# The recurrence of an RWKV layer: both sides of each triangular inverse in different halves of the partitions

## The chip, the cores and the metric

One core of one Trainium2 chip. The time is the device time of one execution in microseconds, lower is better. TensorE (PE) multiplies and transposes; VectorE (DVE), ScalarE (ACT) and GpSimd (POOL) work elementwise; SyncE (SP) issues most DMAs. All data is float32. SBUF has 128 partitions; results of TensorE land in PSUM, 8 banks of 512 columns per partition.

## The reference, cut to what matters

The whole model is a gated MLP layer with a mixture of experts, an RWKV layer with another, and two attention layers. The change touches only the recurrence of the RWKV layer, 512 tokens behind a context of 256, 16 heads of 64, forward and backward in time:

```python
def _wkv_step(S, inp):
    r_t, w_t, k_t, v_t, a_t, b_t = inp
    sa = jnp.einsum('zbhvk,zbhk->zbhv', S, a_t)
    S = S * w_t[..., None, :] + sa[..., :, None] * b_t[..., None, :] + v_t[..., :, None] * k_t[..., None, :]
    return S, jnp.einsum('zbhvk,zbhk->zbhv', S, r_t)
```

## The kernel before, in words

The 768 steps are cut into 12 chunks of 64 tokens. Inside a chunk the steps become products of 64x64 matrices, of which one is the inverse of a unit triangular matrix 1 - L. From chunk to chunk only a linear step of the 64x64 state is left.

`recurrence` (L1269) works two heads at a time (128 channels fill the 128 partitions), in eight calls of `two_heads`. Each call runs three streams of work, interleaved by hand:

- **`chunks` (L1648)**, the matrices of this pair of heads, in three rounds of two tiles of 128 tokens: round 0 the context (tiles 4 and 5, without outputs), rounds 1 and 2 the latent tiles. A round covers 2 directions x 2 tiles x 2 chunks x 2 heads = 16 matrices of 64x64. `units` are the four (direction, tile), `quads` the four (head, chunk).
- **`Prepare` (L1317)**, for the next pair: small products with the LoRA weights, sigmoids, cumulated sums, exponentials, normalised keys. Each engine has a generator of steps (`on_tensor`, `on_scalar`, `on_vector`, `on_pool`), and `chunks` takes one step at each `next(ahead)`.
- **`Scan` (L1539)**, for the pair before: 12 state steps (`next(behind)`), then y is transposed, copied by ScalarE (L1633) and stored by SyncE (L1578).

The first call has no scan, the last no preparation; `Prepare.alone` comes before all, `Scan.alone` after. Every engine executes its own list in order, so a step that waits holds up all that is queued behind it. `Turns` only counts semaphores. At the end of a call all engines meet, and semaphores are cleared.

A round of `chunks`: the products P1 (L and r by b, L1707), XA (L transposed, L1713) and P2 (with k, L1719) go to PSUM and are masked by VectorE (L1832, L1836, L1840). GpSimd masks out of L the quarter of level 1 (L1925) and of level 0 (L1926), and adds the identity (L1929) to both sides of the inverse, `XX`: side 0 holds X, side 1 its transpose. Then five levels double the size of the inverted blocks, 2 to 64. In each, per head:

- Z = quarter of L by X, 8 products (L1745), copied out by ScalarE (L1891, a helper at L1875);
- the update, X side 0 by Z (L1753) and Z by X side 1 (L1756), 8 products each, in level 5 only the second;
- VectorE adds the result to both sides (L1847).

Meanwhile GpSimd makes the quarters two levels ahead (L1934). A product of two 64-row operands uses one 64x64 tile of the array; which one is set by the half of the partitions that its operands lie in and the half that its result goes to. Before, a chunk `cc` of a tile keeps to its own half throughout (`row[cc]`), so operands and result lie in the same half. Ahead of the levels stand the transposes of a and b (L1727) and M.V (L1733); behind them those of k (L1774), then W and U (L1781, copied by ScalarE), Q (L1789), G (L1796, L1798), y's part inside the chunk (L1806, L1808) and F (L1815). VectorE scales Q and G (L1856, L1859) and adds the identity to F (L1866). The scan's step is 4 products of F and the state (L1593), taken up by L1619, and 4 that read y (L1601, added at L1628).

In the profile a float32 product counts as two records of MATMUL and two of LDWEIGHTS (8 products are "x16"); a transpose is one.

## Time and profile before

| | |
|---|---|
| runs | 4815.3, 4812.1, 4813.68 us; median 4813.68 |
| the profiled execution | 4814.21 us, its span 4812.3 us |
| granted clock of TensorE, mean | 0.895 |
| TensorE busy | 3984.3 us (83%) |
| VectorE, ScalarE, GpSimd busy | 1266.8, 819.4, 557.9 us |
| the eight calls of `two_heads` | from 2083.8 to about 2906 us of the span |

The span is from the first to the last instruction of the program in the profile; the time of an execution has little around it. "L1745" is line 1745 of the kernel. An idle time stands in brackets with the one that ended it; "issue" is time in which the engine waited for nothing that the profile shows. The granted clock is a share of 2.4 GHz, the other level is 1.2 GHz.

### The profile page before, as it was taken

Reading aid. Unit: us, or ns where it says so; the run is one execution under the profiler, and the core shown is the slowest. Engines: PE = TensorE matmul, PEld = TensorE weight load, DVE = VectorE, ACT = ScalarE, POOL = GpSimd, SP = SyncE. Lnnn points to the kernel's source line nnn. Section 1 sums busy time; section 2 is a strip of 40 time slices with the busy share of each in tenths; the row PEclk is TensorE's granted clock in tenths of the full one; section 3 lists DMA queues with packets and bytes.
Section 4 is the critical chain, followed back from the end, with each engine's and each line's share of the span. In section 5 each row is a group of like instructions: output and inputs, shape, how many; then the busy total and the mean of one; then the engine's idle time right before and its main releaser. Section 6 shows DMA issues by size and latency. Waiting matters only on the chain. (4 is left out here: it accounts for less than half of the span.)

```text
span 4812.3 us, 71623 instructions
## 1 busy us (share of the span) xinstructions
PE 3984.3 (83%) x30390; PEld 2332.4 (48%) x30390; DVE 1266.8 (26%) x2657; ACT 819.4 (17%) x1707; POOL 557.9 (12%) x718
## 2 busy tenths in 40 slices
PE   4599993699999469878888887579999939997787
PEld 1245542344444235557777773334444414464454
DVE  0213102100000250055455554310000020252174
ACT  0101001011111010143333421001111110231142
POOL 0000000110110000054443530011111100000000
PEclk8799995799999779989999997689999979857999
DMA  8411114388888432200000002348888823201100
GB/s 348 180 53 61 48 35 150 122 331 328 319 330 326 154 90 90 71 14 16 27 16 16 16 6 111 133 177 328 331 318 329 331 102 93 83 1 45 35 36 22
DMA packets 284408, 676.85 MB, mean 141 GB/s; under 512 B 23693, under 2 KB 46829, under 8 KB 283500
## 3 DMA queue, kind: packets, MB, share of 16 engines
q1 hardware_dynamic: 255260, 586.42, 33.6%
q0 software_dynamic: 20928, 71.68, 3.9%
q10 hardware_dynamic: 7952, 14.81, 0.8%
q8 instruction: 213, 3.49, 0.3%
q14 instruction: 55, 0.45, 0.0%
HBM read 618.19 MB, written 54.77 MB: 140 GB/s over the span
## 5 line engine op out<-in xcount | busy, mean ns | idle before, releaser
L862 PE MATMUL banks<-w_gate_ring,x_turned 128*128 128x512 f32 x1024 | 460.0, 602 | 15.3 <-DVE x_turned L934 15.3
L891 PE MATMUL banks<-w_down_ring,hidden_turned 128*128 128x512 f32 x1024 | 450.1, 592 | 1.4 <-ACT hidden_turned L915 1.4
L869 PE MATMUL banks<-w_up_ring,x_turned 128*128 128x512 f32 x1024 | 449.9, 592 | 0.0
L891 PEld LDWEIGHTS banks<-w_down_ring,hidden_turned 128*128 128x128 f32 x1024 | 194.4, 190 | 245.8 <-issue 243.9
L869 PEld LDWEIGHTS banks<-w_up_ring,x_turned 128*128 128x128 f32 x1024 | 194.6, 190 | 244.9 <-issue 244.9
L862 PEld LDWEIGHTS banks<-w_gate_ring,x_turned 128*128 128x128 f32 x1024 | 190.7, 191 | 247.2 <-issue 216.3
L945 DVE COPY y_out_rows<-banks 128x512 f32<-128x512 f32 x64 | 44.3, 692 | 890.9 <-PE banks L891 890.9
L345 PE MATMUL banks<-const_cols,h_tokens 128*128 128x128 f32 x240 | 54.0, 404 | 221.9 <-DVE h_tokens L328 147.0
L1847 DVE TENSOR_TENSOR inverse_both_ways<-banks,inverse_both_ways 128x512 f32<-128x512 f32 (+1 forms) x240 | 152.3, 637 | 252.1 <-PE banks L1756 251.2
L1745 PE MATMUL banks<-inverse_both_ways,l_quarters 64*64 64x64 f32 x3840 | 150.1, 224 | 32.0 <-POOL inverse_both_ways L1929 24.2
L438 PE MATMUL banks<-gmlp_weights,h_turned_gmlp 128*128 128x512 f32 x384 | 166.5, 596 | 11.1 <-DMA gmlp_weights<-in_ga_w_in_dram 11.1
L580 PE MATMUL banks<-gmlp_weights,u_channels 128*128 128x512 f32 x384 | 165.1, 592 | 0.8 <-DVE u_channels L546 0.8
L458 PE MATMUL banks<-h_turned_gmlp,gmlp_weights 128*128 128x384 f32 x512 | 165.3, 486 | 0.0
L1264 PE MATMUL banks<-mixed,proj_weights 128*128 128x384 f32 x512 | 165.3, 486 | 0.0
L345 PEld LDWEIGHTS banks<-const_cols,h_tokens 128*128 128x128 f32 x240 | 44.4, 213 | 234.1 <-DVE h_tokens L328 156.8
L1745 PEld LDWEIGHTS banks<-inverse_both_ways,l_quarters 64*64 64x64 f32 x3840 | 129.9, 136 | 57.4 <-POOL inverse_both_ways L1929 27.3
L843 POOL DMA_INDIRECT y_rows<-y_out_rows,put_rows x64 | 63.2, 987 | 802.8 <-DVE y_out_rows L945 802.8
L939 DVE TENSOR_TENSOR hidden<-silu_gate,banks 128x512 f32<-128x512 f32 x64 | 44.0, 687 | 414.4 <-PE banks L869 414.4
L1756 PE MATMUL banks<-inverse_both_ways,step 64*64 64x64 f32 x3840 | 152.8, 220 | 0.3
L1875 ACT ACTIVATE step<-banks 128x256 f32<-128x256 f32 x240 | 92.2, 384 | 271.1 <-PE banks L1745 265.7
L1756 PEld LDWEIGHTS banks<-inverse_both_ways,step 64*64 64x64 f32 x3840 | 132.4, 136 | 3.2 <-ACT step L1875 2.6
L857 PE MATMUL banks<-const_cols,x_rows 128*128 128x128 f32 x512 | 68.2, 277 | 78.5 <-DMA x_rows<-h_rows,take_rows 78.5
(429 smaller groups left out, 5692.0 us busy)
## 6 DMA issues: line engine op xcount, KB each, us to landing
w_gate_ring<-in_moe_w_gate_dram SPq DMA_DIRECT2D x64, 2048.0 KB, 14.2
w_up_ring<-in_moe_w_up_dram SPq DMA_DIRECT2D x64, 2048.0 KB, 14.4
w_down_ring<-in_moe_w_down_dram SPq DMA_DIRECT2D x64, 2048.0 KB, 9.7
ada_ring<-in_ada_w_dram SPq DMA_DIRECT2D x12, 4096.0 KB, 23.6
gmlp_weights<-in_ga_w_in_dram SPq DMA_DIRECT2D x8, 2048.0 KB, 8.0
ab_weights<-in_ab_w_in_dram SPq DMA_DIRECT2D x6, 2048.0 KB, 8.6
y_back<-y_rows SPq DMA_DIRECT2D x10, 1024.0 KB, 5.2
gmlp_weights<-in_ga_w_out_dram SPq DMA_DIRECT2D x4, 2048.0 KB, 8.1
```

Of the source, the lines that this page charges most:

```text
L345: last = pe.transpose(core.ps[:, 2 * (j % 2) + half, k * P:(k + 1) * P], h[:, j % 2, c0:c0 + P], core.c("ident"))
L438: last = pe.matmul(core.ps[:, step % 8, :], hT[:, k, t * P:(t + 1) * P], wring[:, i % 2, k, :], start=k == 0, stop=k == KD - 1)
L458: last = pe.matmul(core.ps[:, (step + 4) % 8, 0:TOK], wring[:, i % 2, k, m * P:(m + 1) * P], hT[:, k, half * TOK:(half + 1) * TOK], start= ...
L580: last = pe.matmul(core.ps[:, bank, :], uT[:, rest * KD + k, t * P:(t + 1) * P], wring[:, rest, k, :], start=rest == 0 and k == 0, stop=re ...
L862: last = pe.matmul(ps[:, G, :], xT[:, r, k, :], wg[:, r, k, :], start=k == 0, stop=k == KD - 1)
L869: last = pe.matmul(ps[:, U, :], xT[:, r, k, :], wu[:, r, k, :], start=k == 0, stop=k == KD - 1)
L891: last = pe.matmul(ps[:, Y + half, :], hT[:, k, :], wd[:, r, k, half * HALF:(half + 1) * HALF], start=k == 0, stop=k == KF - 1)
L1264: last = pe.matmul(ps[:, i % 8, 0:HT2], wring[:, n % 2, k, m * P:(m + 1) * P], mix[:, j % 2, k, half * HT2:(half + 1) * HT2], start=k == 0 ...
L1745: last = pe.matmul(ps[row[cc], 4 * h + 1, u * CHUNK:(u + 1) * CHUNK], LQ[h][row[cc], n % 2, u, :], XX[h][row[cc], 0, u, :], start=True, st ...
L1756: last = pe.matmul(ps[row[cc], 4 * h, (4 + u) * CHUNK:(5 + u) * CHUNK], Z[h][row[cc], u, :], XX[h][row[cc], 1, u, :], start=True, stop=True)
L1847: DVE.mark(dve.tensor_tensor(x, ps[:, 4 * h, at], x, ALU.add), by_dve, f"XX{n}_{h}")
L1875: copy = lambda dst, src: act.activation(dst, src, ACT.Copy)
```

## The change

In head `h` and chunk `cc`, L and side 0 of the inverse now lie in the half `to_row(h, cc) = row[cc ^ h]`, side 1 and Z in the other, `from_row`. The first product of an update then crosses from one half to the other, the second stays, and with both chunks the four tiles are used in turn. Side 1 gets its product in bank 4h+1, side 0 in bank 4h. L, X and its transpose come from three sets of products (XL, XA, XM). ScalarE copies L unmasked, and GpSimd makes all five masked quarters at the start of a round, each in a buffer of its own. The level-0 inverse is not built: `XI` keeps the identity from the first call on, and VectorE overwrites the entries of the level-0 quarters alone, with predicated copies. r by b becomes products of its own beside level 1, masked after level 2. Other work moves between the levels: a transposed by products with the identity (level 1), b and k transposed (level 3), M.V (level 4). W and U are four tiles wide and copied by two engines. F is copied without the identity, and the scan adds the state by products with the identity (`unit`). In the calls the scan reads y into the free half of bank 3, and `Prepare` keeps to bank 7, one product at a time. Its steps are dealt anew to the levels, and the copy of y for the store comes last on ScalarE. The core of the diff ("..." marks what is left out):

```diff
 class Prepare, on_tensor
+        lag = 2 if self.spare != 7 else 1
         ...
-                if n or z:
-                    pe.wait_ge(s["sig_done"], 2 * (2 * n + z))
                 for half in range(2):
-                    pe.matmul(ps[:, 2 + 4 * half, 0:H2], w[part, :], ...
-                yield
+                    done = 4 * n + 2 * z + half
+                    if done >= lag:
+                        pe.wait_ge(s["sig_done"], done - lag + 1)
+                    pe.matmul(ps[:, (7, self.spare)[half], 0:H2], w[part, :], ...
+                    yield
         ...
-        for t in range(NTA):
-            last = pe.transpose(ps[:, 2 + 4 * (t // 3), ...
+        for half in range(2):
+            if half:
+                pe.wait_ge(s["kk_unit"], 1)
+            for t in range(NTA // 2):
+                ...
+            yield
 class Scan, on_tensor
                     for h in range(2):
-                        last = pe.matmul(ps[row[h], 3, z * CHUNK:(z + 1) * CHUNK], b["F"][row[h], z, ch, :], S[row[h], z, j % 2, :], start=True, stop=True)
+                        pe.matmul(ps[row[h], 3, at], b["F"][row[h], z, ch, :], S[row[h], z, j % 2, :], start=True, stop=False)
+                    for h in range(2):
+                        last = pe.matmul(ps[row[h], 3, at], self.unit[row[h], :], S[row[h], z, j % 2, :], start=False, stop=True)
 chunks
+        to_row = lambda h, cc: row[cc ^ h]
+        from_row = lambda h, cc: row[cc ^ h ^ 1]
 on TensorE
+                    wait(by_act, ACTS, "YC", 1)
+                    ... XA: ps[to_row(h, cc), 4 * h + 1, u * CHUNK:(u + 1) * CHUNK], a by b
+                    ... XM: ps[from_row(h, cc), 4 * h + 1, (4 + u) * CHUNK:(5 + u) * CHUNK], b by a
                     wait(by_dve, DVE, "QG", 1)
+                    ... XL: ps[to_row(h, cc), 4 * h, u * CHUNK:(u + 1) * CHUNK], b by a
+                    wait(by_act, ACTS, "F", 1)
                     ... P2, as before
                     for n in lv:
+                        X = XI if n == 1 else XX
                         for h in range(2):
+                            wait(by_dve, DVE, f"XM_{h}" if n == 1 else f"XX{n - 1}_{h}")
+                            wait(by_pool, POOL, f"LQ{n}_{h}")
                             for u in range(4):
                                 for cc in range(2):
+                                    last = pe.matmul(ps[from_row(h, cc), 4 * h + 1, u * CHUNK:(u + 1) * CHUNK], LQ[h][to_row(h, cc), n - 1, u, :],
+                                                     X[h][to_row(h, cc), 0, u, :], start=True, stop=True)
+                        if rnd == 0 and n < 5:
+                            next(ahead, None)
                         for h in range(2):
                             wait(by_act, ACTS, f"Z{n}_{h}")
                             for u in range(4):
                                 for cc in range(2):
+                                    here = from_row(h, cc)
+                                    if n < last_lv:
+                                        pe.matmul(ps[to_row(h, cc), 4 * h, u * CHUNK:(u + 1) * CHUNK], X[h][here, 1, u, :], Z[h][here, u, :], start=True, stop=True)
+                                    last = pe.matmul(ps[here, 4 * h + 1, (4 + u) * CHUNK:(5 + u) * CHUNK], Z[h][here, u, :], X[h][here, 1, u, :], start=True, stop=True)
+                        if n == 1:
+                            ... (waits MR_0, MR_1; a by identity, and if lat b by r: 16 products each) TA
+                        if n == 3:
+                            ... (waits TA copied, RB) transposes of b into bank 2: TB; of k into bank 6: TK
+                        if n == 4:
+                            ... (waits TK copied) MV, from row[cc] to from_row(h, cc)
                         next(behind, None)
+                        if (rnd == 0 and n < 5) or (rnd == 1 and n in (1, 3, 4)):
                             next(ahead, None)
+                    ... WU, 16 products from from_row(h, cc) to row[cc]
+                    if rnd == 2:
+                        next(ahead, None)
+                    wait(by_act, ACTS, "WU_0")
+                    wait(by_dve, DVE, "WU_1")
                     ... Q, G, YC, F as before (RB in place of LR)
 on VectorE
+                if not scan:
+                    for h in range(2):
+                        dve.tensor_copy(XI[h][:, :, :, :].rearrange("p a u c -> p (a u) c"), c_("ident64").unsqueeze(1).to_broadcast([P, 8, CHUNK]))
                     for h in range(2):
+                        dve.wait_ge(products, PE.of("XM", rnd))
+                        DVE.mark(dve.copy_predicated(by_dir(XI[h][:, 0, :, :]), both("x0", 2, CHUNK).bitcast(U32), by_dir(fours(ps[:, 4 * h + 1, low]))), by_dve, f"XA_{h}")
+                        DVE.mark(dve.copy_predicated(by_dir(XI[h][:, 1, :, :]), both("q1_0", 2, CHUNK).bitcast(U32), by_dir(fours(ps[:, 4 * h + 1, high]))), by_dve, f"XM_{h}")
                     ...
+                        if n == 2 and lat: (waits TA copied) RB: two masked products of 256 columns
                         next(behind, None)
-                        if (rnd, n) not in IDLE:
+                        if (rnd == 0 and n > 2) or (rnd == 1 and n > 1) or rnd == 2:
                             next(ahead, None)
+                    dve.wait_ge(products, PE.of("WU", rnd))
+                    DVE.mark(dve.tensor_copy(WU[:, :, :, 1, :], ...), by_dve, "WU_1")
                     ... QG as before, next(ahead); the sum of F and identity gone
 on ScalarE, per round: L_0, L_1 copied; per level Z_0, Z_1, then TA (n=1), TB and TK (n=3), MV (n=4),
+                        next(ahead, None)
+                        if rnd == 0 and n < 5:
+                            next(ahead, None)
+                    ... WU_0, YC, F copied
+                    if rnd < 2:
                         next(ahead, None)
                 run(ahead)
+                if scan:
+                    scan.on_scalar(act)
 on GpSimd
                 for rnd, pair in enumerate(PAIRS):
+                    for n in lv:
+                        for h in range(2):
+                            pool.wait_ge(by_act, ACTS.of(f"L_{h}", rnd))
+                            POOL.mark(pool.tensor_tensor(by_dir(LQ[h][:, n - 1, :, :]), by_dir(L[h][:, :, :]), quarters(n), ALU.mult), by_pool, f"LQ{n}_{h}")
+                    for _ in range((1, 5, 3)[rnd]):
                         next(ahead, None)
```

## Rows read from the trace of the kernel before

**Rows 1.** Windows of two calls: us; busy PE, PEld, DVE, ACT, POOL; granted clock; DMA.

```profile
2501.00:2606.70 105.70, 91.34 (x2538) 81.42 (x2539) 54.76 (x127) 40.96 (x84) 45.01 (x51) 0.95 0.06 18
...
2816.80:2906.00 89.20, 78.63 (x2496) 73.08 (x2496) 40.60 (x108) 23.94 (x59) 28.40 (x42) 0.98 0.02 7
```

**Rows 2.** Timeline: start us, us, engine, line, operation; round 1, up to level 2.

```profile
2539.27 0.86 PEld L1707 LDWEIGHTS banks<-a_and_r,b_scaled 64*64 64x64 f32 x32 [0.22 <-DVE state_addend L1859]
...
2542.17 0.74 DVE L1836 TENSOR_TENSOR inverse_both_ways<-banks,scan_masks 128x256 f32<-128x256 f32 x2
...
2542.47 0.42 PEld L1727 LDWEIGHTS banks<-const_cols,a_and_r 128*128 128x128 f32 x4
...
2544.36 0.64 POOL L1925 TENSOR_TENSOR l_quarters<-l_and_rb,scan_masks 128x256 f32<-128x256 f32 x1
...
2546.81 0.55 PEld L1745 LDWEIGHTS banks<-inverse_both_ways,l_quarters 64*64 64x64 f32 x16 [1.63 <-POOL inverse_both_ways L1929]
...
2550.56 1.01 PEld L1745 LDWEIGHTS banks<-inverse_both_ways,l_quarters 64*64 64x64 f32 x32 [0.17 <-issue]
```

**Rows 3.** Timeline of the last call: a level without preparation.

```profile
2863.43 0.54 PEld L1753 LDWEIGHTS banks<-step,inverse_both_ways 64*64 64x64 f32 x16
...
2864.63 0.69 DVE L1847 TENSOR_TENSOR inverse_both_ways<-banks,inverse_both_ways 128x512 f32<-128x512 f32 x1 [1.23 <-PE banks L1756]
...
2865.29 0.32 PEld L1593 LDWEIGHTS banks<-state,state_factor 64*64 64x64 f32 x8
...
2865.76 1.09 PEld L1745 LDWEIGHTS banks<-inverse_both_ways,l_quarters 64*64 64x64 f32 x32
...
2866.49 0.38 ACT L1875 ACTIVATE step<-banks 128x256 f32<-128x256 f32 x1 [2.57 <-PE banks L1745]
...
2866.93 1.09 PEld L1756 LDWEIGHTS banks<-inverse_both_ways,step 64*64 64x64 f32 x32
```

**Rows 4.** Timeline of a middle call: W and U, then Q and G.

```profile
2565.28 1.72 PEld L1781 LDWEIGHTS banks<-a_and_mv,inverse_both_ways 64*64 64x64 f32 x32 [0.17 <-issue]
...
2567.94 0.56 PEld L1789 LDWEIGHTS banks<-l_and_rb,w_and_u 64*64 64x64 f32 x32 [0.94 <-ACT w_and_u L1875]
...
2568.40 0.21 PEld L1796 LDWEIGHTS banks<-w_and_u,b_tokens 64*64 64x64 f32 x8
```

**Rows 5.** Timeline of round 0 of the same call: levels 2 and 3.

```profile
2513.14 1.74 PEld L1745 LDWEIGHTS banks<-inverse_both_ways,l_quarters 64*64 64x64 f32 x32 [0.55 <-issue]
...
2517.92 1.55 PE L1390 MATMUL banks<-decay_lora,lora_w 64*128 64x384 f32 x4
...
2519.40 1.01 PEld L1745 LDWEIGHTS banks<-inverse_both_ways,l_quarters 64*64 64x64 f32 x32 [0.55 <-issue]
```

**Rows 6.** Timeline of the same call: steps of the preparation.

```profile
2531.90 1.50 PE L1395 MATMUL banks<-scan_masks,x_tokens 128*128 128x2 f32 x12
...
2533.61 1.02 ACT L1428 ACTIVATE x_tokens<-a_gate,params_here 128x768 f32<-128x768 f32 x1
...
2552.16 1.28 ACT L1439 ACT_TABLE_LOAD   x1
...
2558.61 2.59 DVE L1489 TENSOR_TENSOR k_scaled<-x_tokens,exp_minus_cum 128x768 f32<-128x768 f32 x1
```

**Rows 7.** Timeline: from round 1 to round 2.

```profile
2571.97 0.27 PE L1806 MATMUL banks<-l_and_rb,w_and_u 64*64 64x64 f32 x1 [1.59 <-issue]
...
2572.55 0.90 PEld L1707 LDWEIGHTS banks<-a_and_r,b_scaled 64*64 64x64 f32 x32
```

**Rows 8.** Timeline: end of the same call, start of the next.

```profile
2602.20 0.65 PE L1815 MATMUL banks<-b_tokens,w_and_u 64*64 64x64 f32 x32
...
2606.68 0.33 SPq L1373 DMA_DIRECT2D x_tokens<-k_channels  x1
```

**Rows 9.** DMA issues: count, KB each, median us from issue to landing.

```profile
y_rows_rwkv<-y_two_heads SPq DMA_DIRECT2D x8, 256.0 KB, 2.3
```

**Rows 10.** Timeline: a state step of the scan alone.

```profile
2914.34 0.51 PEld L1593 LDWEIGHTS banks<-state,state_factor 64*64 64x64 f32 x8 [0.34 <-DVE state L1619]
```

More of the change, by code:

```diff
@@ L1729, in _ @@
-                    for h in range(2):
-                        wait(by_dve, DVE, f"MR_{h}")
-                        for u, (z, ti) in enumerate(units):
-                            for cc in range(2):
-                                last = pe.matmul(ps[row[cc], 4 * h + 2, u * CHUNK:(u + 1) * CHUNK], MR[h][row[cc], u, 0, :],
-                                                 b["V"][row[cc], pair[ti], h * 64:(h + 1) * 64], start=True, stop=True)
-                        PE.mark(last, products, f"MV_{h}")
@@ new lines, in _ @@
+                        if n == 4:
+                            wait(by_act, ACTS, "TK")
+                            for u, (z, ti) in enumerate(units):
+                                for h, cc in quads:
+                                    last = pe.matmul(ps[from_row(h, cc), 4 * h + 2, u * CHUNK:(u + 1) * CHUNK], MR[h][row[cc], u, 0, :],
+                                                     b["V"][row[cc], pair[ti], h * 64:(h + 1) * 64], start=True, stop=True)
+                            PE.mark(last, products, "MV")
@@ L1785, in _ @@
-                    wait(by_act, ACTS, "WU_1")
+                    for h in range(2):
+                        wait(by_dve, DVE, f"XX{last_lv}_{h}")
+                    wait(by_act, ACTS, "MV")
+                    for u in range(4):
+                        for h, cc in quads:
+                            here = from_row(h, cc)
+                            last = pe.matmul(ps[row[cc], 4 * h + 1, u * P:(u + 1) * P], XX[h][here, 1, u, :],
+                                             AM[h][here, u, :, :].rearrange("p a c -> p (a c)"), start=True, stop=True)
```

305 lines of the change are left out of this document (147 added, 158 removed).

## The prediction

> **What bounds the kernel now.** The windows by call come first: a middle call of `two_heads` lasts 105.7 us with TensorE busy 91.3, VectorE 54.8, ScalarE 41.0 and GpSimd 45.0 [rows 1]. Eight such calls and the two stretches alone make some 885 us of the 4812.3 us span; nothing else is touched. A matrix engine that is busy 86% of a call invites counting columns, so I read the timeline next, to see what each group of products waits for. A level without preparation takes 3.50 us from one update to the next [rows 3]: Z of both heads (from 2865.76, 0.47 us a head), the first head's update 1.17 us after Z began (Z, then ScalarE's copy), both updates 4 x 0.465 = 1.86 us, then the scan step 0.47. TensorE is never idle in it; VectorE's two additions lie beside it. So **inside a level the issue of products binds**, and at the seams (start of a round, W and U, end of a call) a chain over three engines does.
>
> **Durations.** I sum against the profiled execution (span 4812.3, its own time 4814.2); the median of three is 4813.7, 0.5 less, and I use the difference. What a measurement of this kernel can tell from no change is about 0.2%, some 10 us.
>
> **The update.** Products whose operands and results stay in one half of the partitions use two of the four 64x64 tiles and go at 0.47 us for 16 records (two records are one product); those that use all four go at 0.46 us for 32 (2567.94 to 2568.40) [rows 4]. After the change Z is still two wide (both heads use the same two tiles) and the update four wide for levels 1 to 4; level 5 has only the diagonal pair. The level becomes: Z to first update 1.17; the second head's update can't start before its own copy (0.54 later, 1.71); its issue 0.47; the scan step grows from 16 records to 24 by the unit products, 0.70. Sum 2.88, so 0.62 saved, not the 0.93 that the columns say: ScalarE's copy of the second head ends last. VectorE (first addition 0.73 after the update's issue ends its rows, 0.69 each [rows 3]) frees Z at 2.65, in time.
>
> The Trainium skill (TensorEngine Tiling, Restrictions and Gotchas) says that different row tiles can't write one PSUM bank at once; here both row halves write bank 4h. Rows bear on it: the updates of before send both row halves to one bank at 1.86/64 = 0.029 us a record, while full 128-row products of 128 columns take 0.105 each, 0.053 for 64 [rows 2, 3]. Two row halves do share a bank as long as their output halves differ, which the new layout keeps. By the rule the update would stay at 0.93 a head; that is a rival below.
>
> **The seams of a round.** Before, from the first product to Z of the second head 7.54 us, to Z of level 2 11.29 [rows 2], with 1.6 us in GpSimd's quarter and identity additions. After: XA, XM, XL 3 x 0.47; ScalarE copies L at 1.7; the first quarter 0.64 on GpSimd ends at 3.0; VectorE's four predicated copies end by about 3.1. No row shows a predicated copy; the masked product out of PSUM of the same width takes 0.37 [rows 2], the addition over 512 columns 0.69 [rows 3]. I take 0.4, being the same shape and source; at 0.69 each round loses 1.2, 28 us in 24 rounds. Z begins at 3.05, the second at 3.7; update, a and r.b (0.93), scan step: Z of level 2 at 6.9. GpSimd makes all ten quarters by 9 us, ahead of each level, so these cost nothing unless the copy of L is late. Moved into levels: transposes of b and k (0.85) in level 3, M.V (0.47 after 1.14) in level 4. W and U: 1.72 to 0.86, two copies side by side instead of in a row, the k transposes out of the way: 2.66 becomes about 1.8 and 0.45 before it goes. The addition of the identity to F leaves VectorE; it was beside. A round with nothing prepared beside it, now (89.2 - 2.8)/3 = 28.8 (the last call less its end) [rows 1], is laid out anew as 6.9 to Z of level 2, 2.9, 3.7 and 3.3 for levels 2 to 4, and 7.5 from Z of level 5 to F's last product: 24.4 with rounding, **4.4 saved**.
>
> **The middle calls** hold preparation, whose steps were re-dealt. By round:
> - *Round 0*: now 38.2 us (2501.0 to 2539.3) [rows 1, 2]: 12.1 to Z of level 2, 6.3 for level 2, 19.9 the rest [rows 5]. After: level 1 still waits for the cleared state, then a and the table load (1.28) stand before the first sigmoid for which the second lora product waits: 11.2. Level 2: Z 0.93, lora 0.78, update 0.94, scan 0.3, lora 0.78: 3.7. Level 3 puts the copies of b and k (1.2) ahead of the sigmoid: 5.7; level 4 those of M.V: 5.3; level 5 and tail 7.1, the norm product (1.50) and its wait having left. Sum 33.0: -5.2.
> - *Round 1*: now 33.3, with 2.1 in which TensorE waits for nothing in the profile [rows 2, 7]. What is queued where: the norm product 1.4 now ends level 1 and holds Z of level 2; root and gate factor (0.27 + 1.02) sit before the copy of Z2: 0.8. Then ScalarE's widening of the norms (a like pass, 0.9) waits for VectorE's reciprocal, which stands behind both additions, r.b and the scan step of level 2, and **the copy of Z3 stands behind it**: 2.4. In level 3 copies and a factor: 0.3; in level 4 the copies of M.V, table load 1.28 and exp 0.84 delay Z5's copy: 1.4 [rows 6]. In level 5 VectorE's step precedes its copy of U: 1.3. 7.6 of waits, against seams, update and the normal-vector transposes saved (about 7): 33.8, +0.5.
> - *Round 2*: VectorE's steps of 0.95 follow the additions in all five levels; one beside GpSimd takes 2.59 [rows 6]. With r.b in level 2 the addition of level 3 waits 1.1 to 2.6; ScalarE's exps 1.3; the bonus product before Q 0.85. 25.5 and the same kind of wait 1.2, after 30.3 (2572.55 to 2602.85) [rows 7, 8]: -3.5.
> - *End*: the last products end at 2602.85, the next call begins at 2606.68: 3.8 [rows 8]. y's copy and store now follow F: result 0.2, F's two copies 0.8, y's copy 0.6 (as 0.38 for 256 columns [rows 3]), landing 2.3 [rows 9], then the reset of the semaphores, 2.6 as now: 6.5. **+2.7**. Before, the store lay under W and U.
>
> Sum -5.5 a call, six calls: -33. The first call (no scan, no store) -8. The last (no preparation) 3 x 4.4 - 2.7: -11. The scan alone has 11 state steps in one chain; 8 more records each, 0.4 by its groups of 8 [rows 10]: +4.4. Preparation alone: lora products overlapped -3.3, square late +0.9, halves in turn +0.9: -1.5. **Sum -49: 4765 us.** Unknown: predicated copies (0 to +28), stalls where TensorE waits for nothing in the profile, with a tenth more instructions (0 to +12), the re-dealt queues (-45 to +48).
>
> **Rivals.**
> 1. *The queues take turns well.* If the waits of rounds 1 and 2 (7.5 a call) hide, six calls give 45 more: 4720. For: ScalarE is busy 39% of a call. Against: an in-order queue is late wherever the wait stands. 0.15.
> 2. *ScalarE's queue becomes the chain*, the other side. Place: round 1, levels 1 to 4, copies of Z behind preparation. TensorE stops 2 to 3 us at a time; the granted clock was 0.95 over this call [rows 1], and in a stretch at the lower level (1.2 GHz) Z of both heads took 1.74 instead of 1.01, and level 2 of round 0 6.26 [rows 5]. If round 1 and part of round 2 run at that level, 8 more a call, 48 in six: 4813; from 8.2 a call more it is no gain. Range 4803 to 4835. For: the waits above come one after another, and the idle at a call's end grows by 2.7. Against: such low stretches last 4 us now. 0.20.
> 3. *The update is not four wide*, or the array does not use the diagonal and the crossed tiles together: the second update begins at 2.10 and a level takes 1.17 + 2 x 0.93 + 0.70 = 3.73 instead of 2.88, in 4 levels of 24 rounds 82, and W and U 0.86 x 24 = 20: 4867. Against: four-wide groups with the same mix of halves exist [rows 4]. The rule of the Trainium skill (TensorEngine Tiling, Restrictions and Gotchas) is one way to it. 0.05.
>
> **Numbers.** My case 0.60 (4740 to 4785), rival 1 0.15, rival 2 0.20 (0.05 faster, 0.08 within, 0.07 slower), rival 3 0.05. Faster 0.80, same 0.08, slower 0.12. The range goes from 4715 to 4812: it leaves out rival 3, the upper half of rival 2 and a little below rival 1.
>
> **What would show it.** Update groups of 32 records in about 0.5; bare levels in the last call 2.9; Z of level 2 about 7 after the round begins; in round 1 ScalarE's widening waiting on the reciprocal with Z3's copy behind; 6.5 from F to the next call; middle calls near 100, the last near 78. Middle calls at 94 would mean rival 1, at 105 rival 2; updates still 0.93 a head, rival 3. It would be wrong, too, if the predicated copies cost over 0.7.

## The result, and the profile after

The changed kernel takes 4865.5 us (median of four, 4856.2 to 4867.4) against 4814.5 before (4812.1 to 4823.5): a ratio of 1.0099, 95% interval 1.008 to 1.0117. It is **slower by 51 us**, where 49 us faster was forecast; the time lies above the range. The profiled execution took 4866.3, its span 4864.5, TensorE's mean granted clock 0.883 after 0.895.

The page first: busy time by engine and the slices of the span, then the queue that brings TensorE its instructions.

```profile
span 4864.5 us, 77050 instructions
...
PE 3955.8 (81%) x33046; PEld 2284.4 (47%) x33046; DVE 1259.4 (26%) x2667; ACT 830.4 (17%) x1779; POOL 475.1 (10%) x622
...
PEclk8799995799999789888898997679999979857999
...
q8 instruction: 234, 3.83, 0.3%
```

TensorE is busy 28 us less than before and has 2656 records more (two records are a product, and each has its weight load); the span is 52 us longer, so in sum its idle time grew by 81 us. The instruction queue moved 234 packets; before the change it moved 213. The 21 packets more fit the 5312 instructions that TensorE has more (2656 records and their loads) at 256 a packet.

I cut each call into rounds (first product of one to the first of the next) and the end (last product to next call). Means of the six middle calls, us:

| | before | forecast | after | sigmoids first | fast version |
|---|---|---|---|---|---|
| round 0 | 37.7 | 33.0 | **40.9** | 33.8 | 31.1 |
| round 1 | 32.9 | 33.8 | 34.9 | 35.1 | 34.6 |
| round 2 | 30.5 | 26.7 | 29.7 | 29.3 | 29.9 |
| end | 4.1 | 6.5 | 6.7 | 6.7 | 3.9 |
| middle call | 105.2 | 99.7 | **112.2** | 104.8 | 99.5 |
| first call | 101.5 | 93.5 | 104.8 | 92.5 | 93.4 |
| last call | 90.0 | 79 | 93.9 | 93.9 | 85.9 |

(The last two columns are experiments, below: a_sigmoid_first, and the version with three things put back, by its run v_again.) The forecast missed by 12.5 in each of six middle calls (75), 11 in the first and 15 in the last, 101 in all: the whole of the 100 us. Round 0 holds 7.9 of the 12.5, round 2 holds 3.0.

**The level did what was forecast.** ScalarE's copies of Z in the last call, a level without preparation (timeline, ScalarE alone):

```profile
2867.74 0.87 ACT L1917 ACTIVATE step<-banks 128x256 f32<-128x256 f32 x2 [1.05 <-PE banks L1763]
2870.41 0.38 ACT L1917 ACTIVATE step<-banks 128x256 f32<-128x256 f32 x1 [1.81 <-PE banks L1763]
```

2.67 us from level to level (forecast 2.88, before 3.50 [rows 3]); the 64 records of both updates took 1.18 from first start to last end. This is the shortest of the levels of that call. From Z to the next Z, levels 2, 3 and 4 of the last call's three rounds take 3.3, 3.9 and 3.4 us in the mean, where 2.9, 3.7 and 3.3 were laid out. VectorE's predicated copies:

```profile
2633.67 0.44 DVE L1869 COPY_PREDICATED inverse_of_pairs<-scan_masks,banks 128x256 f32<-128x256 uint32 x1 [1.80 <-PE banks L1740]
2634.01 0.43 DVE L1871 COPY_PREDICATED inverse_of_pairs<-scan_masks,banks 128x256 f32<-128x256 uint32 x1
```

0.34 apart: the 0.4 of the sum was right.

**Round 0 did not.** One middle call, level 1 into level 2 (timeline, all engines):

```profile
2639.51 0.66 ACT L1917 ACTIVATE a_and_mv<-banks 128x256 f32<-128x256 f32 x2 [2.06 <-PE banks L1782]
...
2640.18 1.28 ACT L1427 ACT_TABLE_LOAD   x1
...
2640.58 0.28 PE L1611 MATMUL banks<-state,scan_masks 64*64 64x64 f32 x4
...
2641.48 0.58 ACT L1427 ACTIVATE log_decay<-banks,params_here 128x384 f32<-128x384 f32 x1
2642.11 0.50 PEld L1394 LDWEIGHTS banks<-decay_lora,lora_w 64*128 64x128 f32 x2 [1.39 <-ACT log_decay L1427]
2642.11 1.65 PE L1394 MATMUL banks<-decay_lora,lora_w 64*128 64x384 f32 x2 [1.25 <-ACT log_decay L1427]
...
2643.69 1.44 PE L1763 MATMUL banks<-inverse_both_ways,l_quarters 64*64 64x64 f32 x22
```

Read it from the PE row at 2642.11 upwards. The second lora product waits 1.25 us for the first sigmoid; that stands on ScalarE behind the copies of a and the table load; and Z of level 2 stands behind the lora product on TensorE. At that moment, 2642.1 us, the clock goes down. Windows of this call and of the stretches after it (us; busy PE, PEld, DVE, ACT, POOL; granted clock; DMA):

```profile
2631.60:2744.00 112.40, 87.85 (x2874) 74.62 (x2876) 53.35 (x129) 42.50 (x93) 34.80 (x39) 0.89 0.06 17
...
2636.00:2642.00 6.00, 4.11 (x145) 3.20 (x141) 2.15 (x6) 3.23 (x6) 4.95 (x9) 1.00 0.27 85
2642.00:2650.00 8.00, 7.89 (x117) 5.50 (x117) 1.38 (x2) 1.99 (x5) 0.00 (x0) 0.50 0.01 2
2650.00:2659.00 9.00, 9.00 (x112) 6.28 (x114) 1.86 (x4) 2.05 (x5) 0.00 (x0) 0.50 0.01 2
```

At 0.50 (1.2 GHz) TensorE is busy 9.00 us of 9.00 with 112 records: levels 2 to 4 have become TensorE's own time at half the clock. Inside the eight calls the lower level lasts 182 us, before 54; in round 0 of a middle call 17 us, before 6. Calls of the same code differ by it, since one escaped the long stretch (the first row; the other shows a call that did not):

```profile
2523.20:2631.60 108.40, 81.51 (x2870) 70.66 (x2871) 53.17 (x128) 42.19 (x93) 34.87 (x39) 0.96 0.07 18
2743.90:2858.40 114.50, 88.26 (x2870) 75.60 (x2870) 54.23 (x128) 42.34 (x93) 34.88 (x39) 0.87 0.06 17
```

**The seams stop in the middle of a group.** Last call: the products of y behind G; XM of the next round; the scan's step in level 1 of that round (timeline, TensorE among the others):

```profile
2912.85 0.28 PE L1842 MATMUL banks<-r_by_b,w_and_u 64*64 64x64 f32 x3
...
2915.05 0.28 PE L1842 MATMUL banks<-r_by_b,w_and_u 64*64 64x64 f32 x3 [1.92 <-issue]
```

```profile
2917.26 0.28 PE L1740 MATMUL banks<-a_and_r,b_scaled 64*64 64x64 f32 x3
2919.07 0.34 PE L1740 MATMUL banks<-a_and_r,b_scaled 64*64 64x64 f32 x8 [1.52 <-issue]
```

```profile
2924.72 0.22 PE L1609 MATMUL banks<-state,state_factor 64*64 64x64 f32 x1
...
2926.75 0.27 PE L1609 MATMUL banks<-state,state_factor 64*64 64x64 f32 x2 [1.81 <-issue]
```

Three records of one group, 1.92 us of nothing, three more of the same group: no semaphore stands between them and nothing in the profile ends the wait. Counted over the eight calls, such idle time (pieces over 0.35 us) is 57.8 us, before 15.3. The pieces stand 126 to 128 records apart, or a multiple of that: in the last call after records 655, 909, 1163, 1289, 1542, 1795, 1923, 2177, 2556 and 2811. A packet of the instruction queue is 3.83 MB / 234 = 16.4 kB; the Trainium skill (Perfetto Trace Analysis, The 4-stage abstract model) says that an instruction has 64 bytes, so a packet holds 256, and 127 records with their loads are 254 of them. The packets' own times tie the two together: 52 of the 55 pieces end 2.2 to 2.8 us after a packet began, where only some 12% of all records start that long after one; before the change it is all 15 pieces. So TensorE waits for its next packet. In no trace of this study do two packets start closer than 3.22 us, and in the last call they come 3.5 to 5.8 apart, 3.8 in the median. At the fastest of that call (254 records in 7.22 us between two pieces) a record with its load is supplied every 0.0285 us; two tiles wide they take 0.029, four wide 0.0146. I call this theory T1.

It is dear at the seams. "Z of level 2 about 7 after the round begins" was one of the prediction's signs (6.9 in its sum). In the last call it comes 8.5, 9.5 and 10.5 us after the start of rounds 0, 1 and 2, before the change 10.4, 9.6 and 9.7. In rounds 1 and 2 such pieces fill 2.3 and 3.3 us of it; without them it would be 7.2 both times.

**The end** is as forecast (TensorE's last product, y's copy, the store, the next call):

```profile
2737.54 0.66 ACT L1917 ACTIVATE state_factor<-banks 128x256 f32<-128x256 f32 x2 [1.47 <-PE banks L1850]
2738.09 0.60 ACT L1656 ACTIVATE y_two_heads<-banks 128x512 f32<-128x512 f32 x1
2738.78 0.37 SPq L1590 DMA_DIRECT2D y_rows_rwkv<-y_two_heads  x1
2743.88 0.33 SPq L1375 DMA_DIRECT2D x_tokens<-k_channels  x1
```

### The profile page after: what moved, and what is told of

Read it like the earlier page. It is cut to its first block and busy times, and to the rows that moved or that the text cites. A ratio compares the mean times of both kernels' runs of the same rounds, so it can differ in the third digit from the quotient of the medians.

```text
span 4864.5 us, 77050 instructions
## 1 busy us (share of the span) xinstructions
PE 3955.8 (81%) x33046; PEld 2284.4 (47%) x33046; DVE 1259.4 (26%) x2667; ACT 830.4 (17%) x1779; POOL 475.1 (10%) x622
## 3 DMA queue, kind: packets, MB, share of 16 engines
q8 instruction: 234, 3.83, 0.3%
## 5 line engine op out<-in xcount | busy, mean ns | idle before, releaser
L1977 POOL TENSOR_TENSOR l_quarters<-l_rows,scan_masks 128x256 f32<-128x256 f32 x240 | 144.2, 639 | 348.2 <-ACT l_rows L1917 348.2
L438 PE MATMUL banks<-gmlp_weights,h_turned_gmlp 128*128 128x512 f32 x384 | 167.7, 600 | 11.2 <-DMA gmlp_weights<-in_ga_w_in_dram 11.2
L1886 DVE TENSOR_TENSOR inverse_both_ways<-banks,inverse_both_ways 128x512 f32<-128x512 f32 x192 | 114.8, 621 | 209.1 <-PE banks L1775 208.0
L1775 PE MATMUL banks<-inverse_both_ways,step 64*64 64x64 f32 x3072 | 128.8, 238 | 7.4 <-ACT step L1917 6.9
L1763 PE MATMUL banks<-inverse_both_ways,l_quarters 64*64 64x64 f32 x3072 | 125.5, 234 | 8.8 <-issue 6.4
L905 ACT ACTIVATE x_turned<-banks 128x512 f32<-128x512 f32 x64 | 38.2, 597 | 542.4 <-PE banks L857 542.4
L1264 PEld LDWEIGHTS banks<-mixed,proj_weights 128*128 128x128 f32 x512 | 97.3, 190 | 68.1 <-issue 0.5
```

Of the source, the lines that this page charges most:

```text
L438: last = pe.matmul(core.ps[:, step % 8, :], hT[:, k, t * P:(t + 1) * P], wring[:, i % 2, k, :], start=k == 0, stop=k == KD - 1)
L1264: last = pe.matmul(ps[:, i % 8, 0:HT2], wring[:, n % 2, k, m * P:(m + 1) * P], mix[:, j % 2, k, half * HT2:(half + 1) * HT2], start=k == 0 ...
L1763: last = pe.matmul(ps[from_row(h, cc), 4 * h + 1, u * CHUNK:(u + 1) * CHUNK], LQ[h][to_row(h, cc), n - 1, u, :], X[h][to_row(h, cc), 0, u, ...
L1775: last = pe.matmul(ps[here, 4 * h + 1, (4 + u) * CHUNK:(5 + u) * CHUNK], Z[h][here, u, :], X[h][here, 1, u, :], start=True, stop=True)
L1886: DVE.mark(dve.tensor_tensor(flat(XX), sums, flat(XI if n == 1 else XX), ALU.add), by_dve, f"XX{n}_{h}")
L1977: POOL.mark(pool.tensor_tensor(by_dir(LQ[h][:, n - 1, :, :]), by_dir(L[h][:, :, :]), quarters(n), ALU.mult), by_pool, f"LQ{n}_{h}")
```

## The experiments

Ratios are to the kernel before on the same chip; idle by issue and time at the lower clock are sums inside the eight calls of the profiled execution, in us. (The expectation of a_filled says 188 us for the changed kernel: that takes whole stretches that begin in a call; inside the calls it is 182.)

| run | median us | ratio, 95% | idle by issue | lower clock |
|---|---|---|---|---|
| before | 4814.5 | 1 | 15 | 54 |
| the changed kernel | 4865.5 | 1.0099 (1.008 to 1.0117) | 58 | 182 |
| a_store_early | 4842.9 | 1.0048 (1.0031 to 1.0064) | 61 | 160 |
| a_identity_in_f | 4846.2 | 1.0062 (1.0045 to 1.0079) | 51 | 163 |
| **a_sigmoid_first** | 4814.5 | 0.9996 (0.9986 to 1.0005) | 58 | 88 |
| a_filled | 4840.3 | 1.0043 (1.0029 to 1.0057) | 67 | 100 |
| s_two_wide | 4879.3 | 1.0125 (1.0108 to 1.0142) | 31 | 87 |
| s_store | 4792.4 | 0.9937 (0.9924 to 0.995) | 56 | 98 |
| s_identity | 4786.7 | 0.9933 (0.9921 to 0.9945) | 57 | 70 |
| **s_store_identity** | 4771.1 | 0.9908 (0.9892 to 0.9925) | 55 | 53 |
| v_again, v_nops (same program) | 4773.2, 4770.7 | 0.9907, 0.9892 | 55, 52 | 63, 88 |
| v_a_turned | 4768.7 | 0.9891 (0.9877 to 0.9906) | 41 | 116 |
| v_sems | 5042.3 | 1.0466 (1.0452 to 1.048) | 215 | 394 |
| b_tiny | 5021.8 | 1.0417 (1.04 to 1.0435) | 7 | 180 |
| b_tiny_four | 4901.0 | 1.0167 (1.015 to 1.0184) | 19 | 91 |
| b_nops (same program as before) | 4817.1 | 0.9998 (0.9989 to 1.0008) | 18 | 54 |
| b_sems | 5095.2 | 1.0573 (1.0558 to 1.0587) | 188 | 246 |

### 1. ScalarE's order in round 0

> The changed kernel with one thing moved: in round 0 the first sigmoid of a level stands on ScalarE right behind the two copies of Z, ahead of the copies of a, of the tokens and of mv, so that TensorE's second lora product of the level does not wait behind them. Theory T2a (round 0 is late because the two halves of a lora product now share bank 7 and take turns with ScalarE behind the copies; levels 2 to 4 of round 0 take 8.1, 7.1 and 7.9 us in the middle calls, before 6.6, 5.7, 4.9): levels 2 and 4 lose 1 to 2 us each, 2 to 4 us a call, and where the clock then stays at its upper level up to 6; 15 to 35 us in all, to 4830 to 4850 us. Rival T1 (the supply of instructions sets these levels, the order on ScalarE is hidden): within 6 us of the changed kernel, the idle time by issue still near 58 us.

```diff
                             ACTS.mark(copy(Z[h]...), by_act, f"Z{n}_{h}")
+                        if rnd == 0 and n < 5:
+                            next(ahead, None)
                         if n == 1:
                             need("TA")
...
                         next(ahead, None)
-                        if rnd == 0 and n < 5:
-                            next(ahead, None)
```

One line's place gives all 51 us of the loss back: round 0 falls from 40.9 to 33.8 us, 0.8 from the forecast, and the lower clock from 182 to 88 us. The idle time by issue is 58 us as it was, so the rival is out for this part. (15 to 35 us were expected.) The rows that changed (ScalarE, then TensorE):

```profile
2602.72 1.28 ACT L1427 ACT_TABLE_LOAD   x1 [0.51 <-PE banks L1394]
2604.02 0.58 ACT L1427 ACTIVATE log_decay<-banks,params_here 128x384 f32<-128x384 f32 x1
2604.50 0.65 ACT L1917 ACTIVATE a_and_mv<-banks 128x256 f32<-128x256 f32 x2
```

```profile
2605.56 0.91 PE L1394 MATMUL banks<-decay_lora,lora_w 64*128 64x384 f32 x2
```

The table load now lies under TensorE's update and the lora product waits for nobody.

### 2. How much of that is the clock

> The changed kernel (sigmoids late, 4865 us) with six products of 128 columns by the identity put into TensorE's queue at the end of level 1 of round 0, just before the lora product that waits for the late sigmoid; nothing reads them. They fill the 1.25 us in which TensorE is idle there, right before the granted clock goes to its lower level for 13 to 17 us in most calls. If that idleness is what brings the clock down, and the clock what makes levels 2 to 4 late: clock at the lower level in the calls falls from 188 us to about 100, the middle calls from 112.2 to 107 to 109 us, 4825 to 4845 in all. Rival (levels 2 to 4 are late because of the order on ScalarE alone, and the clock falls behind it): the six products cost nothing or some 0.5 us a call, low clock stays near 188 us, 4860 to 4872.

```diff
                         next(behind, None)
+                        if rnd == 0 and n == 1 and prepare:
+                            pe.wait_ge(by_act, ACTS.of("TA", rnd))
+                            for _ in range(6):
+                                pe.matmul(ps[:, 2, 0:P], core.c("ident"), core.c("ident"), start=True, stop=True)
```

```profile
2632.57 1.60 PE L1810 MATMUL banks<-const_cols 128*128 128x128 f32 x12
2634.33 0.91 PE L1394 MATMUL banks<-decay_lora,lora_w 64*128 64x384 f32 x2 [0.16 <-ACT log_decay L1427]
```

Useless products in the place of the wait, with the late sigmoid left where it was: 25 us faster, the lower clock down from 182 to 100 us, middle calls 109.2. The idleness in front of the lora product does bring the clock down, and the clock alone is worth about half of the 51 us, 25 (27 by the ratios, uncertain by 11); the order on ScalarE keeps the other 26. Round 0 of the six middle calls, piece by piece, shows both (means, us; to Z of level 2, then from Z to Z, then the rest):

| round 0 | to Z of level 2 | level 2 | level 3 | level 4 | rest | sum |
|---|---|---|---|---|---|---|
| forecast | 11.2 | 3.7 | 5.7 | 5.3 | 7.1 | 33.0 |
| changed kernel | 12.7 | 7.0 | 8.2 | 5.6 | 7.3 | 40.9 |
| a_filled | 13.2 | 4.3 | 6.2 | 5.6 | 7.3 | 36.6 |
| a_sigmoid_first | 11.4 | 4.8 | 5.5 | 4.8 | 7.3 | 33.8 |

The clock is the 2.7 and 2.0 us of levels 2 and 3 that the useless products give back; the order is the 1.8, 0.7 and 0.8 us by which a_sigmoid_first is still shorter in front of Z of level 2 and in levels 3 and 4.

### 3. The store, and the identity

> The changed kernel with one thing put back: ScalarE copies the turned y after the levels of round 2, as before, and not behind everything else of the call. Theory T3 (the copy and the store of y stand bare at the end of each of the seven calls with a scan, 6.4 to 6.9 us from the last product to the next call against 3.9 to 4.3 before): the tail falls by about 2.5 us a call, in all 15 to 18 us, to 4847 to 4851 us. Rival (the tail is bound by something else, or round 2 pays for the copy in ScalarE's queue): no more than 5 us.

> The changed kernel with one thing put back: VectorE adds the identity to F, and a step of the scan is one product a half instead of two (88 records of TensorE less in each of seven calls). Theory T1 (TensorE is short of instructions: its groups of 256 instructions come no closer than about 3.65 us, and its idle time put down to issue rose from 15.3 to 57.8 us over the eight calls): 88 of the 332 added records go, so about a quarter of the 42 us of added issue time, 10 us, less what F's adds cost in round seams (2 copies of ScalarE change place with 2 adds of VectorE, about nothing): 4853 to 4860 us. Rival (products that stand in gaps cost nothing): within 4 us of the changed kernel.

> The changed kernel with the sigmoids first, and of the other two only the copy of y put back behind the levels of round 2. The clean price of T3 (the bare tail, 2.6 us in each of seven calls): 18 us less than with the sigmoids alone (0.9996 of before), so 0.9959 of before, 4798 us, range 4793 to 4804. Rival (the two put back at once gave 43 us, most of it through the tail): 4785 to 4792.

> The changed kernel with the sigmoids first, and of the other two only the identity back in F. By the difference of the runs so far, 43 less 18, it brings 25 us: 0.9948 of before, 4793 us, range 4787 to 4799. Theory T1 (it brings this through the supply of instructions) wants the idle time by issue down by about as much, from 58 to some 35 us. Rival (it brings it because a step of the scan stands in front of a level's products and is now 16 records shorter, 0.3 us or more in each of some twelve levels a call): idle time by issue stays at 50 to 58 us and the bare levels of the last call are shorter by 0.3 to 0.8 us.

```diff
+                    if rnd == 2 and scan:
+                        scan.on_scalar(act)
                     need("WU")
...
                 run(ahead)
-                if scan:
-                    scan.on_scalar(act)
```

```diff
-  pe.matmul(ps[row[h], 3, at], b["F"]..., S..., start=True, stop=False)
-  last = pe.matmul(ps[row[h], 3, at], self.unit[row[h], :], S..., start=False, stop=True)
+  last = pe.matmul(ps[row[h], 3, at], b["F"]..., S..., start=True, stop=True)
...
+  dve.wait_ge(products, PE.of("F", rnd))
+  last = dve.tensor_tensor(out["F"]..., by_dir(fours(ps[:, 4 * cc + 2, low])), c_("ident64")..., ALU.add)
```

On the changed kernel itself the two gave 23 and 19 us, but their clock moved at the same time (160 and 163 us at the lower level, after 182), so I repeated them on the version with the sigmoids first. There the store gives 0.0059 of the time, 28 us (18 expected; the interval reaches from some 20 to 36), and the identity 0.0063, 30 us (25 expected; some 23 to 38). The profiled executions differ by less, 17 and 23 us, and of the store's they show 2.9 us at the end of each middle call, which is what was expected; the rest of the 28 has no place in the traces. Idle by issue stays at 57 with the identity back: T1 wanted 35, and here the rival is right. The step of the scan stands in front of a level's products and is 8 records shorter (not 16, as the expectation has it). In the last call, where the clock is nearly the same (8.9 and 8.6 us at the lower level), the call is 3.7 us shorter and its idle time by issue only 0.4. ScalarE's copies of Z in its round 0 lie 4.4, 2.7, 4.1 and 3.8 us apart without, and 3.7, 2.7, 3.5 and 2.7 with the identity back: one of the four levels gains nothing. A part of the 30 us can be the clock (88 to 70 us).

> The changed kernel with the sigmoids first, the copy of y back behind the levels of round 2, and the identity back in F on VectorE: three put back at once. Alone they gave, against the changed kernel's 4865, 51, 23 and 19 us, in disturbed measurements of the last two (round 0's low clock came and went). If they add: 4865 - 51 - 18 - 18 = 4778 us, range 4768 to 4795, faster than before by 0.5 to 1%. If round 0 hid part of the two (they share its disturbance): 4795 to 4805.

All three put back: 4771.1 us, 0.9908 of before, **faster than both kernels**; it was run again (below). Middle calls take 99.7 us in this run and 99.5 in the next.

### 4. What four tiles wide is worth

> The changed kernel with the sigmoids first (4814.5 us), and in it the two sides of an inverse put back into the same half of the partitions: the updates and the products of w and u are two tiles wide again, all else as changed. Theory A (four tiles wide brings what was forecast, 0.6 us a level and 0.9 us for w and u): 15 levels and 3 seams in 8 calls give up 0.62 x 120 + 0.9 x 24, some 96 us, where nothing covers it: 4880 to 4915 us. Theory T1 (short supply of instructions takes back most of the gain; idle time by issue is 58 us in this kernel): two wide, a group is no faster than the supply, so the idle time by issue falls to 10 to 25 us and the net loss is 20 to 60 us: 4835 to 4875. Rival (the levels are bound by the copies and adds of other engines in most rounds): within 15 us of 4814.

```diff
-        to_row = lambda h, cc: row[cc ^ h]
-        from_row = lambda h, cc: row[cc ^ h ^ 1]
+        to_row = lambda h, cc: row[cc]
+        from_row = lambda h, cc: row[cc]
```

(The edit of experiment 1 is in it too.) 65 us slower than with the sigmoids first. The two expectations were 66 to 101 for A and 20 to 60 for T1; the run lies on the border, and the profile says why: idle by issue went from 58 to 31, at the same lower clock (88 and 87 us). The last call shows it best: 3.7 us longer, with 8.1 us less idle by issue. If all idle time by issue counts in full, which is not shown, four wide saves some 92 us and pays 27 of them back as waiting for instructions. Expectation A counted 120 levels, but level 5 is two wide in both; with 96 levels it is 81 us. So the gain of the update was no smaller than forecast, gross.

### 5. What an instruction costs

> The kernel before with 22 products of a single column and 32 weight columns put in behind the updates of every level (330 records a call, as many as the change adds to a middle call), where TensorE next waits for VectorE's add; their results are not used. Theory T1 (instructions come at a bounded rate): the extra records use up no array time to speak of, but push the groups of 256 instructions out: idle time by issue rises from about 15 us to 40 to 60 us over the eight calls, and the time by 20 to 45 us, to 4835 to 4860. Rival (instructions are free as long as TensorE waits anyway; the change costs for another reason): the 22 products take 0.3 to 0.6 us behind each update, inside a wait of over 1 us, and the time stays within 8 us of before.

> The kernel before with the same 22 single-column products behind each level's updates (each is two records, so 660 records a call, twice what the change adds; the expectation of the first such run counted them as 330), now dealt in turn to two halves of the rows and two of the columns of the array. In one place they took 0.035 us a record. Theory T1 (a burst faster than 0.0285 us a record empties TensorE's instructions): the burst takes less than 0.035 a record, idle time by issue rises from 15 to over 40 us, and a bare level is no shorter than its 140 records x 0.0285 = 4.0 us. Rival (a record costs its 0.035 us wherever it stands, TensorE's instructions are issued at that rate and no faster): 1.55 us a burst again, the time again near 5022 us, idle time by issue under 10 us.

```diff
+                        for k in range(22):
+                            rows, to = row[k % 2], slice(64 * (k // 2 % 2), 64 * (k // 2 % 2) + 32)
+                            pe.matmul(ps[to, 1 + 4 * (k % 2), 511:512], core.c("ident")[rows, 0:32], core.c("ident")[rows, 0:1], start=True, stop=True)
```

(The first of them had all 22 in one place of the array.) First row one place, second row four:

```profile
2906.58 1.55 PE L1759 MATMUL banks<-const_cols 64*32 64x1 f32 x44
```

```profile
2939.98 0.54 PE L1760 MATMUL banks<-const_cols 64*32 64x1 f32 x44
```

A record of one column is not free: 1.55 us for the 44, 0.035 each, in one tile, and 0.54 us, 0.012 each, dealt over four. The first run was expected to hide its products inside a wait of over 1 us; there is no such wait in a level, the update's end is the end of TensorE's time, and the bare levels grew from 3.3 to 4.9 us. It says nothing on T1, since its groups are slower than the supply and idle by issue fell to 7. The second refutes my stronger form of T1: idle by issue rose by 4 us only, not to 40, with bare levels of 3.9 us. Most bursts of 44 run through; 15 of the 120 are broken by an idle time "issue" (7.2 us in all). So a burst of 44 seldom empties what TensorE holds; the long pieces come in longer ones, as at the seams.

### 6. Fewer and more instructions in the fast version

> The version with all three put back (4771 us, 0.9908 of before), and in it a is turned by four transposes of a whole tile a round instead of by sixteen products with the identity: 84 records of TensorE less a call, 3% of them, and for one of the two heads in the wrong half of the partitions, so that w is not the reference's. Theory T1 (TensorE's groups of 256 instructions come no closer than 3.24 us in any kernel so far, mostly 3.6, and its idle time by issue is 55 us here): 84 records are 2.4 us of supply a call, the time falls by 8 to 19 us, to 4752 to 4763, and the idle time by issue by as much. Rival (the supply has room wherever it is not in a burst, and this group lies beside a wait): within 4 us of 4771.

```diff
-                                for h, cc in quads:
-                                    last = pe.matmul(ps[from_row(h, cc), 4 * h + 2, u * CHUNK:(u + 1) * CHUNK], b["AR"]..., core.c("ident")[row[h], row[h]], ...)
+                                last = pe.transpose(ps[:, 2 + 4 * (u // 2), (u % 2) * P:(u % 2 + 1) * P], b["AR"][:, z, pair[ti], 0, :], core.c("ident"))
```

> The version with the three put back once more, for comparison on one chip: 0.9908 of before, 4770 to 4776 us.

> The version with the three put back (0.9908 of before), and behind the updates of every level 16 instructions of TensorE that do nothing: 240 a call, 1920 in all, seven and a half groups of 256. Theory T1 (the supply of instructions sets the time here, one group of 256 each 3.3 to 3.7 us): a call takes up to 3.3 us more, 15 to 27 us in all, and idle time by issue rises from 55 by about as much. Rival (they stand where TensorE waits for VectorE, and the supply has room over a whole level): within 5 us. Rival 2 (each costs time of its own on TensorE's sequencer): the same amount in both kernels of this pair.

> The kernel before with the same 16 idle instructions behind the updates of every level. Theory T1: its groups of products are no faster than the supply, so it has room: 0 to 8 us more than before, idle time by issue 15 to 22 us. Rival 2 (each costs its own time): as much as in the other kernel of the pair, where that is more than 8 us.

The idle instructions were dropped when the program was built (228 and 213 packets, as without them), so these two are repeats. They give the scatter: the fast version measures 0.9908, 0.9907 and 0.9892 of before. Against that, 0.9891 with 84 records less (and a w that is not the reference's) is no difference that I can claim. But the idle time by issue fell by 11 to 13 us. In the last call, where nothing is prepared and the clock is nearly undisturbed, it fell from 11.4, 10.4 and 11.3 us (the three traces of the fast version) to 4.9, and the call from 87.5, 85.9 and 87.7 to 83.4 us: 3.6 less, where 84 records at 0.0146 are 1.2. In the middle calls the clock took it back, in this one trace: its lower level lasts 15.6 us a call instead of 7.4, 9.1 and 11.2, and they take 100.9 instead of 99.5 to 100.5.

> The version with the three put back (0.9892 and 0.9907 of before in two measurements), and behind the updates of every level 16 increments of a semaphore that nobody reads, on TensorE's queue: 1920 instructions without array time, 235 or 236 packets of the instruction queue instead of 228. Theory T1 (the supply sets the time here): 15 to 27 us more than 4770, and idle time by issue up by about as much. Rival (the supply has room over a level): within 5 us. Rival 2 (each increment costs its own time on TensorE's queue): the same amount in both kernels of the pair.

> The kernel before with the same 16 increments behind the updates of every level. Theory T1: the supply has room here, 0 to 8 us more than before, idle time by issue 15 to 22 us. Rival 2: as much as in the other kernel of the pair, where that is more than 8 us.

Both kernels lose about the same, 270 and 278 us: 0.14 us for each of 1920 increments. In both traces the increments of a group start 0.151 us apart, TensorE stands idle meanwhile (idle by issue 215 and 188 us), and the lower clock lasts 394 and 246 us. That is rival 2, and the pair says nothing on the supply.

## Why the prediction was wrong

- **The update and the level**: right in the mechanism. 2.67 us for the shortest level, 2.88 forecast, both updates in 1.18; the mean of the bare levels 2 to 4 is 0.2 us over the forecast. The rule that the Trainium skill (TensorEngine Tiling, Restrictions and Gotchas) states, different row tiles not in one bank at once, does not show here: the trace disagrees, row halves with different output halves run together (64 records of both updates in 1.18 us, through banks 4h and 4h+1). Rival 3 is out, though the time came near its 4867.
- **Predicated copies** 0.4 (0.34 apart), **end of a call** 6.5 (6.7): right. The sum had the bare end at 2.7 us in each of seven calls, 19 us; removing it gave 28 by the medians and 17 by the profiled executions.
- **Round 0, level by level: the step that failed first.** The text has "then a and the table load (1.28) stand before the first sigmoid for which the second lora product waits" and adds the delays up to 33.0 us. It saw the wait and priced it at the upper clock. It never asked what TensorE's idleness there does to the clock, although rival 2 had just that mechanism, put in round 1. It happens in round 0: 40.9 us a call instead of 33.0 (and 33.8 with the sigmoids first), 41.6 in the first call (29.5 with the sigmoids first), 51 us in all, about 25 of them by the clock (experiment 2) and 26 by the order (experiments 1 and 2 together). Levels 2 and 3 miss by 3.3 and 2.5 us. Even rival 2's range ended at 4835.
- **Bare rounds 24.4 us, round 2 26.7: the second.** Measured in the last call 26.7, 31.7 and 30.6. "Stalls where TensorE waits for nothing in the profile, with a tenth more instructions" stood among the unknowns with 0 to +12 us; they are 42 us more than before. Rounds 1 and 2 of the last call are 13.5 us over the forecast (62.3 against 48.8), and they hold 10.9 us of idle time by issue, in the middle of groups on the chain (the same rounds before: 1.0). [rows 7] showed one such gap of 1.59 us in the row of before, and I counted it as a constant instead of asking what sets it.
- **Unit products**: no miss, but a cost that the sum accepted: 0.70 instead of 0.47 a step (0.23 in 11 steps of seven calls, 18 us) and "+4.4" for the scan alone. Undoing them gave 30 us by the medians, 23 by the profiled executions. The addition to F cost nothing on VectorE ("it was beside"), so that moving it could not pay.
- **Round 1** 33.8: 34.9, 1.1 out.

What stays open: the worth in time of the 42 us. That they can cost time is shown in the last call, and by the 27 us of idle time that s_two_wide wins back; for the middle calls it is only bounded, since each change of TensorE's load moved the clock too. Why the clock stays down in some calls and not in others of the same code is not settled either. Of the 49 us that remain between 4814 and 4765 the table of rounds places 15 in the last call and, over six middle calls, about 16 in round 2, 8 in round 1 and 5 in round 0. The last call's are mostly idle by issue; for the others this is not shown. The fast version ends near the forecast time by luck: it leaves out two costs that the forecast contained, and they cover most of those 49 us.

## What to carry to other kernels

When a step of one engine's queue makes TensorE wait for a microsecond or more, price the wait twice: as itself, and as what follows if the granted clock goes down behind it; look for a window where a busy TensorE does little at 0.50. When products get cheaper by running side by side, count instructions beside columns: here 256 of them never came sooner than 3.2 us, and a gap "issue" inside a group of like products, at equal distances in records, is its mark; the times of the packets of the instruction queue confirm it. And put work that is hidden now last in the list of things to move; here moving the store and the addition to F cost 43 us together (a_sigmoid_first against s_store_identity).

## What the runs showed of the hardware that was not expected

- Groups of 256 TensorE instructions are never fetched closer than 3.22 us in any trace. Most bursts of 44 records at 0.012 us are covered, the long ones at a seam are not; then TensorE stands up to 1.9 us in the changed kernel and 2.2 in the fast version, and goes on 2.2 to 2.8 us after the packet began.
- A record of one column costs 0.035 us with its load in one tile of the array and 0.012 over four. The Trainium skill (TensorE: Matmul & The Clock Gate, Wait — 56ns, not 53.3ns?) gives about 25 ns as the least distance from the start of one matmul to the next, whatever its width; across four tiles the trace shows half of that.
- Semaphore increments as instructions of their own start 0.151 us apart on TensorE's queue; 1920 of them made two kernels 270 and 278 us slower.
- Fewer products may cost clock: with 84 records less a call the lower level lasted 116 us instead of 53 to 88, each in one trace. The mean granted clock of all executions, 0.891 of four against 0.893 of twelve, points the same way, but less far.
